# The order of the two products in a pair: remainder first in every k tile, the first one included

## The reference

```python
proj = jnp.einsum('bsd,dc->bsc', x, w_in[l]).astype(f32)       # 2048 -> 6144 columns
...
attn_out = jnp.einsum('bsc,cd->bsd', mix, w_out[l])            # 2048 -> 2048
x = layer_norm(DEEPNORM_ALPHA * x + attn_out, ln1_g[l], ln1_b[l])
hdn = jnp.square(jax.nn.relu(jnp.einsum('bsd,df->bsf', x, w_ff1[l])))   # 2048 -> 8192
ff_out = jnp.einsum('bsf,fd->bsd', hdn, w_ff2[l])              # 8192 -> 2048
x = layer_norm(DEEPNORM_ALPHA * x + ff_out, ln2_g[l], ln2_b[l])
```

## Time and profile before

| what | value |
|---|---|
| median of three runs | 1092.44 us |
| the profiled execution | 1092.65 us, span 1090.6 us |
| TensorE (PE) busy | 1086.1 us, 5611 products |
| weight loads (PEld) busy | 922.7 us, 5611 |
| VectorE (DVE) busy | 808.7 us |
| ScalarE (ACT) busy | 572.0 us |
| granted TensorE clock, mean | 1.000 |
| mean DMA rate | 196 GB/s |

### The profile page before, as it was taken

One profiled execution on the slowest core, in us unless ns is written; L12 is line 12 of the kernel. 1 busy time (PEld: TensorE's weight loads), 2 busy tenths in 40 slices (PEclk: granted clock), 3 DMA queues, 4 the chain that ended last, 5 costly groups with the idle time before them and its releaser, 6 DMA issues.

```text
span 1090.6 us, 13914 instructions
## 1 busy us (share of the span) xinstructions
PE 1086.1 (100%) x5611; PEld 922.7 (85%) x5611; DVE 808.7 (74%) x890; ACT 572.0 (52%) x723; POOL 21.9 (2%) x43
## 2 busy tenths in 40 slices
PE   9999999999999999999999999999999999999998
PEld 8888888888888888888888888888888888888886
DVE  6587757767656685667699898666676678889998
ACT  6487757665544524445455454344454455454561
POOL 1000000010000000000000000000000000000000
PEclk9999999999999999999999999999999999999999
DMA  8857655557555835665656556466656755655762
GB/s 292 271 178 221 187 187 155 175 171 251 170 161 167 284 108 159 190 193 174 220 185 230 194 193 231 158 192 190 194 174 202 217 179 194 230 195 191 279 223 78
DMA packets 108047, 213.83 MB, mean 196 GB/s; under 512 B 6784, under 2 KB 38016, under 8 KB 107472
## 3 DMA queue, kind: packets, MB, share of 16 engines
q1 hardware_dynamic: 107216, 209.61, 59.9%
q0 software_dynamic: 624, 3.21, 0.9%
q10 hardware_dynamic: 144, 0.13, 0.0%
HBM read 210.83 MB, written 2.10 MB: 195 GB/s over the span
## 4 chain that ended last, share of the span: by engine, by line
PE 98%; DVE 1%; issue 0%; ACT 0%; DVEq 0%
PE low_ps L789 11%; PE low_ps L628 10%; PE high_ps L789 10%; PE high_ps L808 8%; PE high_ps L809 8%; PE high_ps L807 8%; PE low_ps L522 6%; PE low_ps L526 6%; PE low_ps L524 6%; PE low_ps L794 5%; PE low_ps L633 5%; PE high_ps L794 5%; PE low_ps L809 2%; PE low_ps L808 2%; PE low_ps L807 2%; PE high_ps L569 1%
## 5 line engine op out<-in xcount | busy, mean ns | idle before, releaser
L1293 DVE TENSOR_TENSOR w_lo<-w_raw,w_hi 128x1024 fp32r<-128x1024 f32 x175 | 213.3, 1223 | 128.3 <-ACT w_hi L966 127.0
L966 ACT ACTIVATE w_hi<-w_raw 128x1024 fp32r<-128x1024 f32 x175 | 185.3, 1059 | 186.3 <-PE low_ps L526 67.1
L789 PE MATMUL low_ps<-x1T,w_hi 128*128 128x512 f32 x512 | 176.7, 393 | 0.0
L628 PE MATMUL low_ps<-xT,w_hi 128*128 128x512 f32 x448 | 157.2, 396 | 0.0
L789 PE MATMUL high_ps<-x1T,w_hi 128*128 128x512 f32 x448 | 155.0, 394 | 0.0
L794 PE MATMUL low_ps<-x1T,w_lo 128*128 128x256 f32 x512 | 136.9, 278 | 0.0
L1617 DVE TENSOR_TENSOR w_lo<-w_raw,w_hi 128x1024 fp32r<-128x1024 f32 x72 | 87.1, 1223 | 64.6 <-ACT w_hi L1165 64.6
L633 PE MATMUL low_ps<-xT,w_lo 128*128 128x256 f32 x448 | 124.3, 283 | 0.0
L1165 ACT ACTIVATE w_hi<-w_raw 128x1024 fp32r<-128x1024 f32 x72 | 76.1, 1059 | 88.8 <-PE low_ps L789 43.4
L794 PE MATMUL high_ps<-x1T,w_lo 128*128 128x256 f32 x448 | 119.8, 278 | 0.0
L808 PE MATMUL high_ps<-w_lo,hid 128*128 128x512 f32 x290 | 112.4, 388 | 0.0
(11 more groups left out here) (216 smaller groups left out, 1913.7 us busy)
## 6 DMA issues: line engine op xcount, KB each, us to landing
w_raw<-in_w_ff SPq DMA_DIRECT2D x208, 512.0 KB, 4.4
w_raw<-in_w_in SPq DMA_DIRECT2D x93, 512.0 KB, 4.2
more_raw<-in_w_ff SPq DMA_DIRECT2D x42, 512.0 KB, 5.3
w_raw<-in_w_out SPq DMA_DIRECT2D x32, 512.0 KB, 3.7
x_raw<-in_x_turned SPq DMA_DIRECT2D x8, 256.0 KB, 6.3
y<-in_x SPq DMA_DIRECT2D x8, 256.0 KB, 4.7
side_raw<-in_w_ff SPq DMA_DIRECT2D x4, 512.0 KB, 6.7
w_raw<-in_w_in SPq DMA_DIRECT2D x6, 256.0 KB, 5.0
```

The source lines that it names most:

```text
L628: return pe.matmul(banks[:, b, :], w_hi[:, slot, cols], xT[:, t, :, :].rearrange("p h t -> p (h t)"), start=(t == 0), stop=(t == KT - 1))
L789: return pe.matmul(banks[:, b, :], w_hi[:, slot, cols], x1T[:, t, :, :].rearrange("p h t -> p (h t)"), start=(t == 0), stop=(t == KT - 1))
L966: act.activation(w_hi[:, slot, :], w_raw[:, slot, :], ACT.Copy).then_inc(w_rounded, units)
L1293: dve.tensor_tensor(w_lo[:, slot, :], w_raw[:, slot, :], w_hi[:, slot, :].bitcast(F32), ALU.subtract).then_inc(w_split, units)
```

## The change

In each of the three places the condition on t goes. The 256-column product with the remainder comes first in every pair and carries the start flag at t = 0; the 512-column product follows, never carries the start flag, and ends the bank at t = 15. With `skip_group_check=True` the builder doesn't object to a group that is opened by a product over half the bank.

```diff
@@ qk_products
-                if t == 0:
-                    of_hi()
-                    of_lo()
-                else:
-                    of_lo()
-                    ins = of_hi()
+                pe.matmul(banks[:, b, 0:SEQ], w_lo[:, slot, cols], xT[:, t, 0, :], start=(t == 0), stop=False,
+                          skip_group_check=True)
+                ins = pe.matmul(banks[:, b, :], w_hi[:, slot, cols],
+                                xT[:, t, :, :].rearrange("p h t -> p (h t)"), start=False,
+                                stop=(t == KT - 1), skip_group_check=True)
@@ first_queries
-                        if t == 0:
-                            of_hi()
-                            ins = of_lo()
-                        else:
-                            of_lo()
-                            ins = of_hi()
+                        pe.matmul(banks[:, b, 0:SEQ], lo, xT[:, t, 0, :], start=(t == 0), stop=False,
+                                  skip_group_check=True)
+                        ins = pe.matmul(banks[:, b, :], hi,
+                                        xT[:, t, :, :].rearrange("p h t -> p (h t)"), start=False,
+                                        stop=(t == KT - 1), skip_group_check=True)
@@ hidden_unit
-                    if t == 0:
-                        of_hi()
-                        of_lo()
-                    else:
-                        of_lo()
-                        ins = of_hi()
+                    pe.matmul(banks[:, b, 0:SEQ], w_lo[:, slot, cols], x1T[:, t, 0, :], start=(t == 0), stop=False,
+                              skip_group_check=True)
+                    ins = pe.matmul(banks[:, b, :], w_hi[:, slot, cols],
+                                    x1T[:, t, :, :].rearrange("p h t -> p (h t)"), start=False,
+                                    stop=(t == KT - 1), skip_group_check=True)
```

## The result

The changed kernel takes 1096.55 us (median of 6 runs, 1095.85 to 1097.05), the kernel before 1092.49 us in the runs beside it (6 runs): ratio 1.0037, interval 1.0024 to 1.0050. That is 4.1 us slower; 3.65 were forecast. The profiled execution took 1096.27 us, its span is 1094.2 us.

A forecast was written before the change was run, and what follows sets the result against it. TensorE, never waiting, was taken to bound the kernel by the distances between product starts. 3.76 + 0.10 - 0.41 + 0.20 = +3.65 us on 1092.44 gave 1096.1 us, range 1093.4 to 1099.0 us.

The forecast's parts named there:

- What bounds the kernel: Whole kernel: TensorE waits for nothing, so time is the number of products times the distance between their starts.
- The swap itself costs nothing: All three places: moving 92 256-column products ahead of their 512-column partners costs nothing counted alone, within 1 ns a pair.
- Entry: Runs entered with 256 columns behind 512-column products go long, as in `first_queries`; chunks 7 to 15: +3.76 us.
- Chunk 1 and chunks 2 to 6: First feed-forward matrix: chunk 1's first two units long, +0.10 us; chunks 2 to 6 short behind eight transposes, -0.41 us.
- Projection: `qk_products`: first four units go long behind the opening, +0.20 us; the rest taken as 0, expected under 0.7 us.
- The k = 0 units are what resets it: Pace of alternating pairs: a carried state, 346.8 or 353.4 ns a pair, reset by the k = 0 units the change removes.
- the order of a pair is all that matters: Rival, all 92 swaps: under 1 ns each, 0.1 us together, 1092.4 us; within the not-slower cases, 0.16 together.
- a plain alternation settles short: Rival: chunks 1 to 6 -0.41, chunks 7 to 15 -0.04 us; 1092.2 us; within the not-slower cases, 0.16 together.
- Both runs long: Rival: the long pace survives the transposes, so chunks 1 to 6 run long too; +6.08 us, 1098.5 us; chance 0.33.
- The Trainium skill's formula: Every pair: columns at full clock plus about 2.5 ns per product, an estimated 325 ns in either order; change worth nothing.

The follow-up runs named there:

- the run of nine: Not a follow-up run but a stretch: chunks 7 to 15, from the first pair's start to the start of the product behind the last; 199.80 us before the change.
- the mirrored kernel: The changed kernel with the 512-column product first in every pair, in all three places: 1099.40 us, ratio 1.0061 to the kernel before.
- the first experiment: The changed kernel with the old order back at t = 0 of chunk 7 alone: 1092.53 us, ratio 0.9999 to the kernel before.

## Why the prediction was right

**What bounds the kernel:** right. TensorE waits 1.2 us in all, and each stage's length is the sum of the distances between its products' starts.

**The swap itself costs nothing:** right. With 88 of 92 swaps in place and the run of nine short, the kernel runs as before (ratio 0.9999).

**Entry:** right. The run of nine began as the opening's units did, and stayed long for all 576 pairs: 203.52 us against 203.56 forecast. That this would outlast the 56 pairs seen was the step with the least behind it, and it held to the last pair.

**Chunk 1 and chunks 2 to 6:** right in both terms, +0.1 and 110.93 us for 110.98. That the eight transposes bring back the short pace was the one open step, taken at 0.42 against 0.33, and it held: behind them the changed kernel runs as the kernel before does, though it entered them long. The reason given, that TensorE settles into the same state behind equal transposes, fits this and isn't shown. It isn't a rule for every version either: with the large product first behind them, in the mirrored kernel, the run is long.

**Projection:** +0.20 was forecast for the first four units, and 11.30 us stand for 11.31. For the rest 0 was taken and +0.15 came (222.46 against 222.11, less the 0.20), inside the 0.7 allowed. Nothing was worked out there that could have said which way it would go, so that it came so close is luck.

**"The k = 0 units are what resets it":** too simple. A doubled unit turns the long pace into the short one from one point of its cycle in three; from the other two it stays long, and chunk 2's doubled unit even turned the short one into the long. The forecast didn't need more, since it rested on entries and not on resets.

**The measured size:** the spans' difference is 3.6 us and fits the sum term by term; the medians differ by 4.1, within the scatter of the runs (changed 1095.85 to 1097.05).

**The rivals:** "the order of a pair is all that matters" fell with the first experiment, "a plain alternation settles short" with the trace after. "Both runs long" didn't happen here, but did in the mirrored kernel, whose 1099.4 us is near the 1098.5 worked out for it. The Trainium skill's formula ("TensorE: Matmul & The Clock Gate", section "Back-to-back issue gap"), by which the change would be worth nothing, misses both the level (346.7 and 353.3 ns a pair measured, an estimated 325 by the formula) and the memory. The prediction took it for more than it is: the section gives it for a single product alone and says that in a stream of weight loads and products the two together set the distance.

## What to carry to other kernels

Where one engine is busy all the time, look at the distance between starts over long runs, not at the records: two stretches of the same code may differ by 2%, and a small edit at a stage's border can put the whole next stage on the other pace. Before you call such an order harmless, find a stretch in the trace that is entered in the same way as the new one will be, and read the pace there. If the pace depends on how a stretch is entered, an order that breaks up the alternation (large, small, small, large) costs 1.7 ns a pair more than the short pace and saves 4.9 against the long one. That it is right for other sizes than these no run shows.

## What the runs showed of the hardware that wasn't expected

- The same sequence of products (256 and 512 columns in turn, float32r, new weights each time, full clock) has two steady paces, 346.7 and 353.3 ns a pair. Each held without a break for as long as a run lasted: the long one over 576 pairs in four kernels, the short one over 368 (changed kernel, chunks 1 to 6) and 568 (behind the doubled unit of chunk 7).
- The long one is a cycle of three pairs. A doubled unit leads out of it from one of its points and not from the other two, and can also lead from the short pace into it. One turned pair at the start of a run doesn't prevent it.
- Which product opens the bank and carries the start flag doesn't matter for the long pace, nor does exchanging the large products of two banks: 203.52, 203.51 and 203.52 us.
- Eight transposes followed by the small product leave the short pace, whichever came before them: they and the rest of chunk 1 take 17.51 us in the kernel before, entered short, and 17.52 in the changed one, entered long.
- Weight loads of 128 rows and 128 columns overlap (records of 0.19 us), but start no closer than 0.11 us. With a small product of 128 columns the load behind comes 0.05 us late, and the pair takes 340 ns where 293 were worked out from its columns; with 384 columns in the large product it takes 286.7.
- Stays open: what in TensorE makes the cycle of three pairs.
